# Four rotated products into the output product, and a negation on ScalarE, in the S5 scan of layer 0

## The chip, the cores and the metric
One Trainium2 chip, one core of it. The metric is the device time of one execution in microseconds (us), the median of several. Engines: TensorE (PE, with PEld its weight loads), VectorE (DVE), ScalarE (ACT), GpSimd (POOL) and SyncE (SP), which issues the DMAs.

## The reference
A two-layer trunk for 256 tokens of width 1024. The part that the change touches is the S5 mixer of layer 0: 32 groups of 64 complex states, a diagonal recurrence over the tokens, and an output product that takes the real part.

```python
step = jnp.exp(log_step)[:, None]
mag = jnp.exp(lr * step)
ar = mag * jnp.cos(li * step)
ai = mag * jnp.sin(li * step)
...
bu_r = jnp.einsum("bsgh,gph->sbgp", uf, bbr)
bu_i = jnp.einsum("bsgh,gph->sbgp", uf, bbi)
_, _, xr, xi = lax.associative_scan(_complex_combine, (a_r, a_i, bu_r, bu_i), axis=0)
y = (jnp.einsum("sbgp,ghp->bsgh", xr, c_re)
     - jnp.einsum("sbgp,ghp->bsgh", xi, c_im))
y = y + d_skip * uf
y = jax.nn.gelu(y.reshape(bsz, s, S5_WIDTH))
return y * jax.nn.sigmoid(y @ w_glu)
```

## The kernel before
The recurrence is solved in 16 steps (`for q in range(NQ)`), each for two groups, that is 128 states on the partitions and 256 tokens along the row. The complex decay is split into its size and its angle: the inputs are turned back by the angle of their token, a real scan with the size runs over real and imaginary part, and the result is turned forward again. The tables of cosines and sines lie in slots 4 and 5 of the weight ring. All engines run loops of their own over the same 16 steps and meet at semaphores.

- **TensorE.** `s5_in(q)` (L1417) writes the two inputs of a step into a bank, one step ahead. `s5_out(q)` (L1409) multiplies the two state parts with the output weights `ct` and adds them up in one bank over four steps; it waits for `re_ready` and `im_ready`. In iteration q the order is `s5_in(q+1)`, the turn of the previous adaLN row (`ada_turn`, L1313, after its copy on ScalarE and the previous row's sum on VectorE), `s5_out(q-2)`, in iterations 3 to 7 the products of the pooling mixer (L1280), and in iterations 4, 5, 7, 8, 10, 11, 13 and 14 (`ADA_AT`) the product of one adaLN weight tile (`ada_mm`, L1305).
- **VectorE.** Two products of the bank with the tables (L982), a sum and a difference of them (L985, L986), the two scans (L990) into `zz`, then `states(q-1)` (L972), which makes the imaginary part of the step before out of two of GpSimd's products; then, after an adaLN step, `mods` (L826, L829), and in steps 6, 10 and 14 `skip` (L967), which takes the finished bank of four steps. The scans wait until GpSimd is done with step q-2, since `zz` and `qq` have two buffers each.
- **GpSimd.** After both scans of a step, and after `s5_out(q-2)` for its buffer, two products of 128x512 (L531) give four rotated parts of 256 each, and one sum (L534) makes the real part of the state.
- **ScalarE.** Copies only: the pooling mixer's two (L665, L669), the adaLN row (`ada`, L585, which waits for `ada_mm`), and `gelu` (L674) behind `skip` in iterations 6, 10 and 14, with one table load ahead of the first.

The adaLN and the later weight tiles are issued by SP in the order of a list, each as soon as the last user of its ring slot is done; the slots of the tables are refilled after the last rotated product. After the 16 steps follow the last `skip` and `gelu`, the product of the gate (L1280, 32 records, "glu"), the output projection, and the feed-forward part of layer 0.

What a step leaves in `qq` before: with zr, zi the scanned parts and C, S the tables, `qq[k]` holds (zr, zi) times C for k=0 and times S for k=1, and the sum and difference of them are the two state parts.

## Time and profile before

| | |
|---|---|
| median of 3 runs | 1679.56 us (1677.16 to 1680.3) |
| profiled execution, its own time | 1678.3 us |
| span of the profiled execution | 1676.2 us |
| busy over the span | PE 92%, PEld 54%, DVE 26%, ACT 13%, POOL 6% |
| the chain that ended last | PE 80%, DMA 8%, DVE 6%, issue 4%, ACT 1% |
| chain from 81 to 151 us | VectorE, line after line of the scan loop |

The span is what the profiler saw of one execution; 2.1 us of the execution's own time lie around it. The shares of the whole span say little here, since the change lies in some 75 us of it. In that stretch the chain of waits runs through VectorE; ahead of it and behind it it runs through TensorE.

### The profile page before, as it was taken

The page shows a single profiled execution, that of the slowest core. Times are in us where ns is not written, and L with a number is a line of the kernel's source. Part 1 is how long each engine was busy: PE and PEld are TensorE (multiplying, and loading weights), DVE is VectorE, ACT ScalarE, POOL GpSimd, SP SyncE. Part 2 cuts the span into 40 slices and gives each one's busy share as a digit, 9 for nine tenths or more (in the row PEclk, how much of TensorE's full clock was granted, in tenths as well). Part 3 has the DMA queues.
Part 4 walks back from the last instruction along what each step waited for, and adds up shares of the span by engine and source line. Part 5 has one row for each costly group of instructions (what it writes and reads, how often), then busy time and mean ns, then how long its engine had stood idle before and what let it go on. Part 6 is the DMA issues. An engine that isn't in the chain of part 4 may idle for free.

```text
span 1676.2 us, 23905 instructions
## 1 busy us (share of the span) xinstructions
PE 1544.0 (92%) x10681; PEld 906.2 (54%) x10682; DVE 429.9 (26%) x895; ACT 215.0 (13%) x411; POOL 106.1 (6%) x129
## 2 busy tenths in 40 slices
PE   7887999999999999989999998999999889977975
PEld 5644487777588766546343353356666643423322
DVE  6796212232255455222000001010010010100202
ACT  3311300000321143220000000000000000000001
POOL 7164000000000011000000000000000000000000
PEclk9997999999999999998999999999999999999999
DMA  9576386664564403255999986999999969999996
GB/s 339 177 247 236 139 302 244 234 224 169 181 228 151 151 1 143 109 206 216 404 408 409 391 296 259 403 408 408 402 406 395 377 250 404 407 409 403 408 407 240
DMA packets 167297, 485.74 MB, mean 290 GB/s; under 512 B 12928, under 2 KB 15872, under 8 KB 167168
## 3 DMA queue, kind: packets, MB, share of 16 engines
q1 hardware_dynamic: 162624, 482.51, 75.4%
q8 instruction: 103, 1.69, 0.4%
q10 hardware_dynamic: 4544, 1.33, 0.4%
q14 instruction: 26, 0.21, 0.0%
HBM read 482.78 MB, written 1.05 MB: 289 GB/s over the span
## 4 chain that ended last, share of the span: by engine, by line
PE 80%; DMA 8%; DVE 6%; issue 4%; ACT 1%; POOL 0%; DVEq 0%; SPq 0%; POOLq 0%; ACTq 0%
PE bank L1753 26%; PE bank L1280 21%; PE bank L1784 13%; DMA ring<-in_moe_w_down 5%; PE bank L1483 5%; PE bank L1673 3%; DMA ring<-in_moe_w_gate 3%; PE bank L1593 3%; PE bank L1725 2%; PE bank L1287 1%; DVE arena L982 1%; PE bank L1765 1%; PE bank L1632 1%; DVE arena L990 1%; PE bank L1608 1%
## 5 line engine op out<-in xcount | busy, mean ns | idle before, releaser
L1753 PE MATMUL bank<-ring,arena 128*32 128x256 f32 (+3 forms) x3664 | 387.0, 432 | 42.1 <-issue 27.0
L1753 PEld LDWEIGHTS bank<-ring,arena 128*32 128x32 f32 (+1 forms) x3664 | 179.4, 121 | 238.6 <-issue 182.0
L1280 PE MATMUL bank<-arena,ring 128*128 128x256 f32 x1264 | 282.8, 384 | 1.4 <-ACT arena L674 1.0
L1280 PEld LDWEIGHTS bank<-arena,ring 128*128 128x128 f32 x1264 | 240.9, 193 | 34.4 <-ACT arena L674 1.7
L1784 PE MATMUL bank<-ring,arena 128*32 128x256 f32 (+1 forms) x1792 | 208.1, 459 | 16.1 <-DMA ring<-in_moe_w_down 15.3
L1202 DVE TENSOR_TENSOR arena<-arena,bank 128x512 f32<-128x512 f32 (+2 forms) x44 | 24.4, 577 | 658.6 <-PE bank L1753 658.6
L1784 PEld LDWEIGHTS bank<-ring,arena 128*32 128x32 f32 (+1 forms) x1792 | 87.4, 121 | 127.4 <-issue 90.8
L1753 PE MATMUL bank<-arena 128*32 128x256 f32 (+3 forms) x1200 | 116.1, 402 | 9.8 <-issue 4.0
L788 ACT ACTIVATE arena<-bank 128x512 f32<-128x512 f32 (+2 forms) x44 | 21.1, 508 | 645.5 <-PE bank L1765 549.1
L1753 PEld LDWEIGHTS bank<-arena 128*32 128x32 f32 (+1 forms) x1200 | 57.9, 121 | 65.8 <-issue 49.9
L1483 PE MATMUL bank<-ring,arena 128*128 128x512 f32 x176 | 76.9, 595 | 1.5 <-PE bank L1280 1.5
L1593 PE MATMUL bank<-ring,arena 128*128 128x512 f32 x128 | 59.4, 608 | 2.5 <-DVE hd L1098 2.5
L1483 PEld LDWEIGHTS bank<-ring,arena 128*128 128x128 f32 x176 | 33.0, 190 | 42.5 <-issue 42.5
L1673 PE MATMUL bank<-ring,arena 128*128 128x512 f32 x128 | 55.3, 593 | 0.0
L1020 DVE TENSOR_TENSOR arena<-arena,bank 128x256 f32<-128x256 f32 x22 | 9.3, 421 | 160.2 <-PE bank L1280 160.2
L1784 PE MATMUL bank<-arena 128*32 128x256 f32 (+1 forms) x336 | 43.2, 472 | 3.1 <-DMA arena<-in_moe_w_down 3.1
L531 POOL TENSOR_TENSOR arena<-arena,ring 128x512 f32<-128x512 f32 x32 | 41.5, 1316 | 67.0 <-DVE arena L990 59.6
L1188 DVE TENSOR_SCALAR arena<-bank,gs,mod 128x128 f32<-128x128 f32 x64 | 21.9, 404 | 84.7 <-PE bank L1280 84.7
L844 DVE SCALAR_TENSOR_TENSOR arena<-ring,cT,arena 128x512 f32<-128x512 f32 x56 | 42.1, 751 | 1.7
L1280 PE MATMUL bank<-ring,arena 128*128 128x512 f32 x96 | 42.0, 594 | 0.1
L546 POOL TENSOR_TENSOR arena<-arena,hd 128x256 f32<-128x256 f32 x16 | 10.2, 636 | 504.4 <-ACT arena L725 376.6
L556 POOL COPY arena<-arena 128x6 f32<-128x6 f32 x8 | 1.5, 188 | 638.3 <-DVE arena L1179 618.0
(274 smaller groups left out, 1240.5 us busy)
## 6 DMA issues: line engine op xcount, KB each, us to landing
ring<-in_moe_w_down SPq DMA_DIRECT2D x46, 2048.0 KB, 19.3
ring<-in_moe_w_up SPq DMA_DIRECT2D x45, 2048.0 KB, 23.6
ring<-in_moe_w_gate SPq DMA_DIRECT2D x41, 2048.0 KB, 23.7
ring<-in_ada_w SPq DMA_DIRECT2D x24, 2048.0 KB, 9.5
arena<-in_moe_w_gate SPq DMA_DIRECT2D x15, 2048.0 KB, 23.6
ring<-in_m_w_in SPq DMA_DIRECT2D x12, 2048.0 KB, 9.0
arena<-in_moe_w_up SPq DMA_DIRECT2D x11, 2048.0 KB, 23.6
arena<-in_moe_w_down SPq DMA_DIRECT2D x10, 2048.0 KB, 21.7
```

What stands on the lines that cost most here:

```text
L531: c.inc(g.tensor_tensor(qq[:, q % 2, k], zz[:, q % 2], tables[:, 1 - k, q:q + 1, :].broadcast_to([P, 2, TOK]), ALU.mult), "q_ready")
L788: ins = f(sg[:, b, 0:w], ps[b][:, 0:w], ACT.Silu)
L844: c.then(stt(o, w[:, kc], cT[:, kc, 0:1], o, ALU.mult, ALU.add), "ada_summed" if kc == KC - 1 else step)
L1188: ins = ts(hcur3[:, kc], bank(kc // 4, 4, P)[:, kc % 4], gs[:, kc:kc + 1], mod[:, 1, 3, kc:kc + 1], ALU.mult, ALU.add)
L1202: ins = tt(sg[:, b, 0:w], sg[:, b, 0:w], ps[2 + b][:, 0:w], ALU.mult)
L1280: ins = mm(out_, l, r, start=i == 0, stop=i == len(pairs) - 1, **kw)
L1483: ins = mm(ps[i][:, :], act_f[:, t % 2, j, P * b:P * b + P], w[:, j, HALF * h:HALF * h + HALF], start=t == 0 and j == 0, stop=t == 5 and j ...
L1593: ins = mm(ps[6 + zi % 2][:, :], hT[:, kc, P * b:P * b + P], w[:, kc], start=kc == 0, stop=kc == KC - 1)
L1673: ins = mm(ps[4 + i][:, :], yT1[:, 4 * t + j, P * b:P * b + P], w[:, j, HALF * h:HALF * h + HALF], start=t == 0 and j == 0, stop=t == 3 an ...
L1725: mm(ps[banks[i]][:, :], gates[:, P * (i // 2):P * (i // 2) + P], y_sb[:, HALF * (i % 2):HALF * (i % 2) + HALF], start=True, stop=True).th ...
L1753: ins = mm(ps[base + b // per][m * h:m * h + m, w * (b % per):w * (b % per) + w], hcur3[:, kc, m * b:m * b + m], sl[:, kc - half * rows, w ...
L1784: ins = mm(ps[4 + b // per][m * h:m * h + m, w * (b % per):w * (b % per) + w], actT[:, t % 2, b // per, n * (b % per) + i, m * q:m * q + m ...
```

## The change
`zz` becomes two buffers of three parts, (zr, zi, -zr), the third written by ScalarE (`negate`, an ACTIVATE Copy with scale -1). The first rotated product of GpSimd takes (zr, zi), the second (zi, -zr) and waits for the negation. The four results need no sum or difference any more: TensorE multiplies each with its weights and adds all four in the bank, four products a step where there were two. The sum on GpSimd (L534) and the difference on VectorE (L972) go, with their semaphores. `s5_out` waits for the two rotated products.

```diff
-        zz = area(16384, 2, 2, TOK)
+        zz = area(7424, 3, TOK), area(16384, 3, TOK)
...
                 for k in range(2):
-                    c.inc(g.tensor_tensor(qq[:, q % 2, k], zz[:, q % 2],
+                    if k:
+                        pool.wait_ge(s["neg_ready"], q + 1)
+                    c.inc(g.tensor_tensor(qq[:, q % 2, k], zz[q % 2][:, k:k + 2],
                                           tables[:, 1 - k, q:q + 1, :].broadcast_to([P, 2, TOK]), ALU.mult), "q_ready")
-                pool.wait_ge(s["q_ready"], 2 * q + 2)
-                c.inc(g.tensor_tensor(qq[:, q % 2, 0, 0], qq[:, q % 2, 0, 0], qq[:, q % 2, 1, 1], ALU.add), "re_ready")
...
+            def negate(q):
+
+                act.wait_ge(s["z_ready"], 2 * q + 1)
+                if q >= 2:
+                    act.wait_ge(s["q_ready"], 2 * (q - 1))
+                c.inc(f(zz[q % 2][:, 2], zz[q % 2][:, 0], ACT.Copy, scale=-1.0), "neg_ready")
             for q in range(NQ):
+                if q:
+                    negate(q - 1)
...
                 if q in (6, 10, 14):
                     gelu((q - 6) // 4)
+            negate(NQ - 1)
             gelu(3)
...
-            def states(q):
-
-                dve.wait_ge(s["q_ready"], 2 * q + 2)
-                c.inc(tt(qq[:, q % 2, 0, 1], qq[:, q % 2, 0, 1], qq[:, q % 2, 1, 0], ALU.subtract), "im_ready")
...
-                if q:
-                    states(q - 1)
...
-                pe.wait_ge(s["re_ready"], q + 1)
-                pe.wait_ge(s["im_ready"], q + 1)
+                pe.wait_ge(s["q_ready"], 2 * (q + 1))
...
                 for i in range(2):
-                    ins = mm(ps[4 + m % 2][:, 0:TOK], ct[:, q, i], z[:, 0, i], start=q % 4 == 0 and i == 0,
-                             stop=q % 4 == 3 and i == 1)
+                    for k, part in enumerate((z[:, 0, i], z[:, 1, i])):
+                        ins = mm(ps[4 + m % 2][:, 0:TOK], ct[:, q, i], part, start=q % 4 == 0 and i == 0 and k == 0,
+                                 stop=q % 4 == 3 and i == 1 and k == 1)
```

On ScalarE `negate(q-1)` stands at the head of iteration q, so `negate(q)` is queued behind all that iteration q holds. The rows from iteration 3 to the first `gelu` (iteration 6) and one row beyond, before, where L665 and L669 are the pooling mixer's copies and L585 the copy of an adaLN row:

```order
L665 ACTIVATE arena<-bank0 128x256
L669 ACTIVATE arena<-bank0,cols 128x256
L665 ACTIVATE arena<-bank1 128x256
L585 ACTIVATE arena<-bank6 128x512
L669 ACTIVATE arena<-bank1,cols 128x256
L665 ACTIVATE arena<-bank0 128x256
L585 ACTIVATE arena<-bank6 128x512
L669 ACTIVATE arena<-bank0,cols 128x256
L665 ACTIVATE arena<-bank1 128x256
L674 ACT_TABLE_LOAD
L674 ACTIVATE arena<-arena 128x256
L669 ACTIVATE arena<-bank1,cols 128x256
```

and now, from the copy of iteration 4 on:

```order
L585 ACTIVATE arena<-bank6 128x512
L680 ACTIVATE arena<-arena 128x256
L669 ACTIVATE arena<-bank1,cols 128x256
L665 ACTIVATE arena<-bank0 128x256
L585 ACTIVATE arena<-bank6 128x512
L680 ACTIVATE arena<-arena 128x256
L669 ACTIVATE arena<-bank0,cols 128x256
L665 ACTIVATE arena<-bank1 128x256
L674 ACT_TABLE_LOAD
L674 ACTIVATE arena<-arena 128x256
L680 ACTIVATE arena<-arena 128x256
L669 ACTIVATE arena<-bank1,cols 128x256
```

Each L680 is a negation. Those of steps 4 and 5 stand behind the adaLN copies (L585) of iterations 4 and 5, that of step 6 behind the first `gelu`. No table load is added.

On GpSimd the first two steps and the start of the third, before:

```order
L531 TENSOR_TENSOR arena<-arena,ring 128x512 [waits z_ready,tab_sin,band_ready]
L531 TENSOR_TENSOR arena<-arena,ring 128x512
L534 TENSOR_TENSOR arena<-arena 128x256 [waits q_ready]
L531 TENSOR_TENSOR arena<-arena,ring 128x512 [waits z_ready]
L531 TENSOR_TENSOR arena<-arena,ring 128x512
L534 TENSOR_TENSOR arena<-arena 128x256 [waits q_ready]
L531 TENSOR_TENSOR arena<-arena,ring 128x512 [waits y_mm,z_ready]
```

and now:

```order
L533 TENSOR_TENSOR arena<-arena,ring 128x512 [waits z_ready,tab_sin,band_ready]
L533 TENSOR_TENSOR arena<-arena,ring 128x512 [waits neg_ready]
L533 TENSOR_TENSOR arena<-arena,ring 128x512 [waits z_ready]
L533 TENSOR_TENSOR arena<-arena,ring 128x512 [waits neg_ready]
L533 TENSOR_TENSOR arena<-arena,ring 128x512 [waits y_mm,z_ready]
```

Two instructions a step in place of three, the second with a wait of its own. On TensorE iteration 4 (`s5_in(5)`, `s5_out(2)`, pooling, `ada_mm`), before:

```order
L1417 MATMUL bank3<-arena,ring 128x256 [waits bu_used]
L1417 MATMUL bank3<-arena,ring 128x256
L1409 MATMUL bank4<-arena 128x256 [waits im_ready,re_ready]
L1409 MATMUL bank4<-arena 128x256
L1280 MATMUL bank0<-arena 128x256 [waits pool_in_ready]
L1280 MATMUL bank1<-arena 128x256 x2
L1305 MATMUL bank6<-ring,cT 32x512 [waits ring_full2,ada_copied]
```

and now:

```order
L1419 MATMUL bank3<-arena,ring 128x256 [waits bu_used]
L1419 MATMUL bank3<-arena,ring 128x256
L1411 MATMUL bank4<-arena 128x256 [waits q_ready]
L1411 MATMUL bank4<-arena 128x256 x3
L1282 MATMUL bank0<-arena 128x256 [waits pool_in_ready]
L1282 MATMUL bank1<-arena 128x256 x2
L1307 MATMUL bank6<-ring,cT 32x512 [waits ring_full2,ada_copied]
```

The adaLN product, for which ScalarE's copy waits, stands behind two more products of 128x256.

## Rows read from the trace of the kernel before

**Rows 1.** Windows: length; busy (count) of PE, PEld, DVE, ACT, POOL; clock; DMA.
```profile
82.30:151.50 69.20, 53.02 (x288) 30.85 (x286) 67.62 (x108) 10.63 (x20) 43.65 (x40) 0.93 0.66 231
```

**Rows 2.** Timeline of DVE: start, length (us), line, operation, [idle before <-releaser].
```profile
86.19 1.68 DVE L990 TENSOR_TENSOR_SCAN arena<-hd,arena 128x256 f32<-128x256 f32 x2
...
108.86 0.40 DVE L972 TENSOR_TENSOR arena<-arena 128x256 f32<-128x256 f32 x1
109.18 1.41 DVE L982 TENSOR_TENSOR arena<-bank,ring 128x512 f32<-128x512 f32 x2
110.62 1.29 DVE L985 TENSOR_TENSOR arena<-arena 128x256 f32<-128x256 f32 x1
111.84 0.95 DVE L986 TENSOR_TENSOR arena<-arena 128x256 f32<-128x256 f32 x1
112.82 1.27 DVE L990 TENSOR_TENSOR_SCAN arena<-hd,arena 128x256 f32<-128x256 f32 x2
...
114.53 1.02 DVE L829 TENSOR_TENSOR mod<-modraw,cols 128x4 f32<-128x4 f32 x1
...
116.91 0.94 DVE L985 TENSOR_TENSOR arena<-arena 128x256 f32<-128x256 f32 x1
...
118.22 1.27 DVE L990 TENSOR_TENSOR_SCAN arena<-hd,arena 128x256 f32<-128x256 f32 x2
```

**Rows 3.** Timeline of POOL beside them.
```profile
109.03 2.61 POOL L531 TENSOR_TENSOR arena<-arena,ring 128x512 f32<-128x512 f32 x2 [2.00 <-DVE arena L990]
111.71 0.79 POOL L534 TENSOR_TENSOR arena<-arena 128x256 f32<-128x256 f32 x1
114.23 2.54 POOL L531 TENSOR_TENSOR arena<-arena,ring 128x512 f32<-128x512 f32 x2 [1.73 <-issue]
116.84 0.72 POOL L534 TENSOR_TENSOR arena<-arena 128x256 f32<-128x256 f32 x1
```

**Rows 4.** Timeline of DVE, step 15, which comes late enough to find POOL idle.
```profile
147.38 0.47 DVE L967 SCALAR_TENSOR_TENSOR arena<-arena,cols,bank 128x256 f32<-128x256 f32 x1
...
149.21 0.55 DVE L985 TENSOR_TENSOR arena<-arena 128x256 f32<-128x256 f32 x1
149.69 0.41 DVE L986 TENSOR_TENSOR arena<-arena 128x256 f32<-128x256 f32 x1
150.13 1.27 DVE L990 TENSOR_TENSOR_SCAN arena<-hd,arena 128x256 f32<-128x256 f32 x2
```

**Rows 5.** Timeline of PE, iteration 5.
```profile
93.92 1.03 PE L1409 MATMUL bank<-arena 128*128 128x256 f32 x4
94.78 1.46 PE L1280 MATMUL bank<-arena 128*128 128x256 f32 x6
96.17 1.92 PE L1305 MATMUL bank<-ring,cT 128*32 128x512 f32 x16
```

**Rows 6.** Timeline of ACT, iterations 5 and 6.
```profile
98.16 0.60 ACT L585 ACTIVATE arena<-bank 128x512 f32<-128x512 f32 x1 [1.50 <-PE bank L1305]
...
102.97 1.28 ACT L674 ACT_TABLE_LOAD   x1
105.42 0.42 ACT L674 ACTIVATE arena<-arena 128x256 f32<-128x256 f32 x1 [1.16 <-DVE arena L967]
```

**Rows 7.** Timeline of DVE and PE at the end of the loop and behind it.
```profile
147.60 0.63 PE L1313 MATMUL bank<-ident,arena 128*128 128x128 f32 x4 [3.37 <-DVE mod L829]
...
154.17 0.98 DVE L972 TENSOR_TENSOR arena<-arena 128x256 f32<-128x256 f32 x1 [1.30 <-POOL arena L531]
155.29 2.04 PE L1409 MATMUL bank<-arena 128*128 128x256 f32 x4 [1.38 <-DVE arena L972]
...
158.36 9.12 PE L1280 MATMUL bank<-arena,ring 128*128 128x256 f32 x32 [1.02 <-ACT arena L674]
```

**Rows 8.** Windows of PE: length, busy (count), clock, DMA share, GB/s.
```profile
148.00:149.00 1.00, 1.00 (x7) 0.84 0.00 0
162.00:163.00 1.00, 1.00 (x5) 0.83 1.05 387
```

More of the change, by code:

```diff
@@ L279, in hybrid_trunk @@
             xn_ready turned hT_low hT_high gs_ready u_mm u_ready pool_mm pool_in_ready pool_out_mm pool_out
-            bu_mm bu_used z_ready q_ready re_ready im_ready y_mm yskip ys_ready glu_mm glu_sig yT_ready gg_ready grow_mm grow_ready
+            bu_mm bu_used z_ready neg_ready q_ready y_mm yskip ys_ready glu_mm glu_sig yT_ready gg_ready grow_mm grow_ready
             sq_done rg_ready root_in root_done xroot_done out_mm x_ready dve_step             f_mm f_silu f_act
@@ L989, in _ @@
                 for k in range(2):
-                    c.inc(v.tensor_tensor_scan(zz[:, q % 2, k], prm[:, MAG, q:q + 1].broadcast_to([P, TOK]), t[:, k, 0],
+                    c.inc(v.tensor_tensor_scan(zz[q % 2][:, k], prm[:, MAG, q:q + 1].broadcast_to([P, TOK]), t[:, k, 0],
                                                0.0, ALU.mult, ALU.add), "z_ready")
-                if q:
-                    states(q - 1)
                 if q - 1 in ADA_AT:
@@ L998, in _ @@
                 dve.wait_ge(s["z_ready"], 2 * (q + 1))
-            states(NQ - 1)
             skip(3)
```

## Prediction

> **What bounds the kernel now.** The reader first looks at the chain of waits, which goes through VectorE from 81 to 151 us, and at the windows of that stretch: of 69.20 us VectorE is busy 67.62, TensorE 53.02, GpSimd 43.65, ScalarE 10.63 [rows 1]. So the scan loop ends when VectorE ends, and TensorE has 16 us to spare.
>
> Next comes the timeline of VectorE, to see of what a step consists. I call T(q) the end of step q's second scan. T(3) is 87.87 and T(15) 151.40 [rows 2, 4], 63.5 us for 12 steps, 5.3 each. From T(7)=108.95 to T(8)=114.09 it takes: L972 up to 109.18, the table products (L982) 1.44, L985 1.22, L986 0.98, the scans 1.27 [rows 2]. Where GpSimd is idle, L985 takes 0.48 and L986 0.44 [rows 4]. The difference is waiting: L985, queued at 110.62, ends as GpSimd's second product does (109.03 + 2.61 = 111.64), and L986 as its sum does (111.71 + 0.79 = 112.50) [rows 2, 3]. L829, a sum of 4 columns, takes 1.02 and ends with the first product; L982, which reads a bank, doesn't wait at all. So an operation of VectorE with both inputs in SBUF waits for the instruction that GpSimd has running, and the port is handed over between two instructions. This is the rule of the Trainium skill ("SBUF — State Buffer", Who interferes with whom): such an instruction contends with GpSimd's reads, and who comes first blocks the other for the whole instruction. These rows agree (1.29 where 0.48 is free).
>
> **Part 1: L534 and L972 go.** A step without `mods` is then: table products up to T+1.4; L985 waits for the second product, which ends at T+2.7, and is done at T+2.9; L986 0.44, scans 1.3: 4.63 in place of 5.14, a gain of 0.51. A step with `mods`: L829 waits for the first product up to T+1.4 whether L972 stood ahead of it or not, so L972's time there was hidden; table products to 2.8, when GpSimd is done; L985 0.48, L986 0.44, scans 1.3: 5.03 against 5.40 (114.09 to 119.49), a gain of 0.37, which is L534's block alone. Twelve intervals, seven with `mods`: 5 x 0.51 + 7 x 0.37 = 5.1 us, if nothing takes their place.
>
> **Part 2: the negation.** The trace has no such instruction; the nearest are L674 at 0.42 for 128x256 (SBUF to SBUF) and L585 at 0.60 for twice as much [rows 6]; I take 0.42 and 0.05 for each handover. It can start after the first scan, at T-0.65, and GpSimd needs it at T+1.35. It costs nothing as long as ScalarE is free by T+0.9. Queued ahead of it are:
> - `gelu` in steps 6, 10 and 14, behind `skip`. With `mods` (6, 14) `skip` ends at T+1.9 (0.47, rows 4), gelu at 2.35, the negation at 2.8, the second product at 4.15. L985, ready at 3.3, waits up to 4.3, and the step takes 6.05: 0.65 more than before instead of 0.37 less. Two of them cost 2 x 1.0 = 2.0. Step 10 has no `mods`, its negation is 0.05 late: 0.1.
> - the adaLN copy in eight steps, which waits for TensorE.
>
> **Part 3: TensorE.** `s5_out` takes 0.86 for two products (93.92 to 94.78) and `s5_in`, of the same shape and number, as much [rows 5]; four products take 1.72. Sixteen more times 0.86 are 13.8 us in a stretch where 16 are idle, so the averages say that it fits, but order counts. In its favour, `s5_out(q-2)` needn't wait for L972, which ran only after the next scans, so it may start 2.3 us earlier. After the long input projection TensorE starts behind: it ends `s5_out(0)` at 83.8, then s5_in 0.86, s5_out 1.72, pooling 0.86, s5_in, s5_out(2) to 89.8, pooling 1.4, `ada_mm` 1.85 up to 93.05 [durations from rows 5]. The copy ends at 93.75 and step 4's negation at 94.15, with T(4)=92.55: late by 0.25. The next round is 0.95+0.45+1.72+1.3+1.85, so `ada_mm` ends at 99.35, copy 100.05, negation 100.45, with T(5)=97.15: the second product is late by 1.9. VectorE has done its table products, L985 and L986 at 100.9; the product then takes the port up to 102.2, and the scans end at T(6)=103.35 (before 103.54, so the gain up to there is 0.2). Then step 6 with its gelu, whose table load (1.28, rows 6) now comes later, since it stands behind a pooling copy that ends at 104.25: negation 106.35, T(7)=109.65, 0.7 behind the kernel before. GpSimd starts step 7 late for the same reason: T(8)=114.35, 0.25 behind.
>
> From here TensorE keeps up (copy of step 8 ends at T(8), of 11 at T(11)-1.0), and the gains of part 1 add up: steps 8 and 9 to 124.4 (0.5 ahead), 10 to 129.1 (0.95), 11 and 12 to 139.16 (1.7), 13 to 143.8 (2.2), 14 with gelu to T(15)=149.8, **1.6 ahead**.
>
> **Part 4: the tail.** Before, GpSimd's products end 2.65 after T(15), L972 takes 0.98 (it waits for L534) and 1.1 in all, then s5_out(15) 2.04 at half clock up to 157.35 [rows 7], 5.95 after T(15). Now L972 goes and the products double: 149.8 + 2.9 = 152.7, and then between 1.9 (full clock) and 3.8 (half). Before, the clock fell to half at about 148.7, just after a gap of 3.37 us that ended at 147.60, and rose at about 162.3 [rows 7, 8]. Now TensorE idles from 142.1 to 145.3, works 4 us with a half us between, and idles 3.0 again, so I take half clock: end 156.5, **0.85 ahead**. The gate product took 9.12 for 32 records [rows 7], where at the full rate of 0.215 a record (four in 0.86, rows 5) it takes 6.9: a clock that rises earlier by virtue of the longer s5_out(15) gives back 0 to 2.2; I take 1.1.
>
> Sum: 0.85 + 1.1 = 1.95. Nothing behind absorbs it: the output projection and the feed-forward part are TensorE's chain, their tiles are issued when a slot or the tables come free, which moves by as much. The adaLN tiles of this stretch land before use (`ring_full` releases no matmul here). Start of the loop: the negations of steps 0 and 1 stand behind the copies L679 at 73.3 and 81.0; GpSimd gets them by 82.0, VectorE's step 3 starts at 82.3 with its bank anyway, and s5_out(1) at 84.6. Cost nothing, and if that cover failed, 0.3 us. `zz` at 7424 covers nothing that is alive.
>
> The profiled execution took 1678.3 (span 1676.2), 1.26 below the median; taken off its own time the sum gives 1676.3, taken off the median **1677.6**, which I forecast.
>
> **Rivals.**
> 1. *The clock holds through the tail.* s5_out(15) 1.9 instead of 3.8 and the gate product at full rate: 1.9 + 1.1 more, a gain of 5.0, **1674.6**. For it: TensorE has more work in every gap. Against it: the 3.0 us gap just ahead. Chance 0.20.
> 2. *A scan goes ahead of the late product.* In steps 5 and 6 I let the product have the port after L986. If the first scan, queued right behind, keeps it, the scans are through 1.15 earlier in step 5 and about 0.9 in step 6: a gain of 4.0, **1675.6**. The rows show the port handed to a waiting VectorE instruction between two of GpSimd's, never the reverse. Chance 0.15. By the Trainium skill (the section named above) the first to start holds the port, which leaves this case open, since both are ready at once.
> 3. *The negation is late in all adaLN steps.* The copy must end by T+0.9. By my account step 8 has 1.0 us of margin and step 11 1.9. If TensorE falls to half clock for some us, as it did somewhere in the loop before (mean clock 0.93, rows 1), or the round is 1 us longer than summed, the second product moves in front of the scans instead of lying beside the table products, at 6.2 - 5.03 = 1.2 a step; six more steps cost 7.2, a loss of 5.2, **1684.8**. It decides from a copy that ends later than T+0.9. Against it: TensorE no longer waits for L972. Chance 0.13.
> 4. *The blocks only move.* Each of VectorE's small operations finds a product running anyway, because GpSimd starts late for want of its buffer: loop even, tail 0.75 worse, **1680.3**. Chance 0.07.
>
> **How the numbers follow.** Forecast 0.45, held inside 1676.2 to 1680. A measurement can tell about 0.2% (3.4 us) from no change. Faster by more than that (below 1676.2): rivals 1 and 2, 0.35, and 0.02 of the forecast's edge: 0.37. Slower (above 1682.9): rival 3, 0.13. The rest, 0.50, is within. The range goes from rivals 1 and 2 together (1679.56 - 7.05 = 1672.5) to 1682.5, which leaves out most of rival 3 and a little below: 0.18 in all.
>
> **What would show it.** In the timeline of the changed kernel: steps without `mods` of 4.6 us and with them of 5.0 (part 1); steps 5, 6 and 14 of 6 us or more, with the second product away from the first by 1 to 2 us (parts 2, 3); T(15) near 149.8; s5_out(15) of 3.8 at a granted clock of 0.5. Wrong: a gap between the two products in steps 8 to 13 (rival 3), a last s5_out of 1.9 (rival 1), a scan running while GpSimd's second product is ready and waits (rival 2), or L985 above 0.5 in the steps with `mods` (part 1).

## The result and the profile after

The changed kernel took **1669.11 us** in the median of 5 runs (1665.53 to 1670.13), the kernel before 1679.56 in 5 runs of the same series (1677.16 to 1681.11): ratio 0.9939, interval 0.9928 to 0.9950, so faster by 0.6%. A second series gave 1671.17 (1668.82 to 1671.77) against 1679.6, ratio 0.9948 (0.9931 to 0.9965). The forecast of 1677.6 had the sign of its sum right and the size wrong by 8.5 us, and its range (1672.5 to 1682.5) did not reach the result. The profiled execution took 1668.35, with a span of 1666.5 against 1676.2 before. One run of this study, one of the five of the kernel with the sum alone, took 2157.58 us at a mean granted clock of 0.70; its ratio leaves it out.

Windows of the scan loop in the kernel after, from the table products of step 3 up to the end of step 15. The columns are those of [rows 1]: length; busy (count) of PE, PEld, DVE, ACT, POOL; clock; DMA share; GB/s.

```profile
85.66:150.80 65.14, 61.65 (x352) 41.77 (x350) 63.42 (x96) 15.15 (x33) 34.30 (x27) 1.00 0.70 245
```

VectorE is still the engine that is always busy (63.42 of 65.14), GpSimd has lost its third instruction, and the granted clock is 1.00 where it was 0.93 [rows 1]. The loop from T(3) to T(15) takes 59.50 where it took 63.53.

Timeline of VectorE in the kernel after: from T(7) to T(8) without `mods`, and from 130.96 on T(11) to T(12), with `mods`. Columns as in [rows 2].

```profile
112.36 1.42 DVE L987 TENSOR_TENSOR arena<-bank,ring 128x512 f32<-128x512 f32 x2
113.81 1.37 DVE L990 TENSOR_TENSOR arena<-arena 128x256 f32<-128x256 f32 x1
115.11 0.41 DVE L991 TENSOR_TENSOR arena<-arena 128x256 f32<-128x256 f32 x1
115.56 1.27 DVE L995 TENSOR_TENSOR_SCAN arena<-hd,arena 128x256 f32<-128x256 f32 x2
...
130.96 1.26 DVE L838 TENSOR_TENSOR mod<-modraw,cols 128x4 f32<-128x4 f32 x1
132.15 1.40 DVE L987 TENSOR_TENSOR arena<-bank,ring 128x512 f32<-128x512 f32 x2
133.58 0.42 DVE L990 TENSOR_TENSOR arena<-arena 128x256 f32<-128x256 f32 x1
133.92 0.42 DVE L991 TENSOR_TENSOR arena<-arena 128x256 f32<-128x256 f32 x1
134.38 1.27 DVE L995 TENSOR_TENSOR_SCAN arena<-hd,arena 128x256 f32<-128x256 f32 x2
```

L990 and L991 are the lines that were L985 and L986. L838 is the sum of 4 columns that was L829, and L987 the table products, L982 before. Without `mods`, the first still waits for GpSimd's second product (1.37, where [rows 2] have 1.29) and the second runs free at 0.41 where it took 0.98, since no sum follows on GpSimd. With `mods`, both are free at 0.42, and it is the sum of 4 columns (L838) that waits, 1.26. The steps last 4.50 and 4.79, where they lasted 5.14 and 5.40.

Timeline of TensorE at the end of the loop in the kernel after, to be held against [rows 7].

```profile
142.33 1.92 PE L1307 MATMUL bank<-ring,cT 128*32 128x512 f32 x16
146.46 0.63 PE L1315 MATMUL bank<-ident,arena 128*128 128x128 f32 x4 [2.21 <-DVE mod L838]
146.92 3.93 PE L1411 MATMUL bank<-arena 128*128 128x256 f32 x16
153.34 2.00 PE L1411 MATMUL bank<-arena 128*128 128x256 f32 x8 [2.48 <-POOL arena L533]
156.42 7.17 PE L1282 MATMUL bank<-arena,ring 128*128 128x256 f32 x32 [1.09 <-ACT arena L674]
```

The last `s5_out` has 8 records in 2.00, where it had 4 in 2.04, and the gate product takes 7.17 where it took 9.12. TensorE runs at 2.4 GHz here throughout. The windows of TensorE from 120 to 165 us show it (length, busy (count), granted clock, DMA share, GB/s), first of the kernel after:

```profile
120.00:165.00 45.00, 37.93 (x214) 1.00 0.71 249
```

and the same of the kernel before:

```profile
120.00:165.00 45.00, 33.71 (x150) 0.77 0.58 202
```

**Where the 9.7 us of span went.** I use three marks: T(0), the end of the first step's scans; T(15); and F, the first matmul of the feed-forward part behind the gate, at which the code is again the same in both kernels.

| us | T(0) | T(0) to T(3) | T(3) to T(15) | T(15) to F | T(0) to F | F to the end |
|---|---|---|---|---|---|---|
| before | 68.9 | 18.96 | 63.53 | 54.45 | 136.94 | 1470.4 |
| before, second trace | 71.1 | 18.97 | 63.53 | 54.43 | 136.93 | 1470.5 |
| after | 72.3 | 18.96 | 59.50 | 51.25 | 129.71 | 1464.5 |
| after, second trace | 71.9 | 18.95 | 59.50 | 51.24 | 129.69 | 1467.8 |

The head of the program, which the change leaves alone, happened to be 3.35 longer in the first trace of after (T(0) lies between 68.6 and 72.3 in all traces of this study). The loop gives 4.0, the tail 3.2, together 7.2 us, repeated to 0.02. The rest, 5.9 in the first pair of traces and 2.7 in the second, lies in code that is the same in both kernels. So there are two questions: why the changed stretch gives 7.2 and not the 1.95 forecast, and why the code behind it got shorter.

### The profile page after: what moved, and what is told of

Its sections match the earlier page's. It is cut to its first block, busy times and chain, and to the rows that moved or that the text cites. A ratio compares the mean times of both kernels' runs of the same rounds, so it can differ in the third digit from the quotient of the medians.

```text
span 1666.5 us, 24017 instructions
## 1 busy us (share of the span) xinstructions
PE 1547.8 (93%) x10745; PEld 913.0 (55%) x10746; DVE 421.0 (25%) x879; ACT 220.3 (13%) x427; POOL 93.5 (6%) x113
## 4 chain that ended last, share of the span: by engine, by line
PE 77%; DMA 8%; issue 2%; DVE 2%; ACT 1%; POOL 0%; DVEq 0%; SPq 0%
PE bank L1755 26%; PE bank L1282 20%; PE bank L1786 13%; DMA ring<-in_moe_w_down 5%; PE bank L1485 5%; PE bank L1675 3%; DMA ring<-in_moe_w_gate 3%; PE bank L1595 3%; PE bank L1727 2%; PE bank L1767 1%; PE bank L1634 1%; PE bank L1610 1%; PE bank L1330 1%; PE bank L1296 0%; PE bank L1475 0%
## 5 line engine op out<-in xcount | busy, mean ns | idle before, releaser
L1485 PEld LDWEIGHTS bank<-ring,arena 128*128 128x128 f32 x176 | 33.0, 190 | 42.5 <-issue 42.5
L1675 PEld LDWEIGHTS bank<-ring,arena 128*128 128x128 f32 x128 | 24.2, 191 | 29.6 <-issue 29.6
L1595 PEld LDWEIGHTS bank<-ring,arena 128*128 128x128 f32 x128 | 23.8, 196 | 26.8 <-issue 26.8
```

Of the source, the lines that this page charges most:

```text
L1485: ins = mm(ps[i][:, :], act_f[:, t % 2, j, P * b:P * b + P], w[:, j, HALF * h:HALF * h + HALF], start=t == 0 and j == 0, stop=t == 5 and j ...
L1595: ins = mm(ps[6 + zi % 2][:, :], hT[:, kc, P * b:P * b + P], w[:, kc], start=kc == 0, stop=kc == KC - 1)
L1675: ins = mm(ps[4 + i][:, :], yT1[:, 4 * t + j, P * b:P * b + P], w[:, j, HALF * h:HALF * h + HALF], start=t == 0 and j == 0, stop=t == 3 an ...
```

## The experiments

**One add at a time, and none.** The first kernel leaves only the sum to TensorE. It is the kernel before with

```diff
-                pool.wait_ge(s["q_ready"], 2 * q + 2)
-                c.inc(g.tensor_tensor(qq[:, q % 2, 0, 0], ..., ALU.add), "re_ready")
...
-                for i in range(2):
-                    ins = mm(..., ct[:, q, i], z[:, 0, i], ...)
+                for n, (i, part) in enumerate(((0, z[:, 0, 0]), (0, z[:, 1, 1]), (1, z[:, 0, 1]))):
+                    ins = mm(..., ct[:, q, i], part, ...)
```

> Only GpSimd's sum goes: TensorE takes its two terms as two products (three a step), VectorE keeps the difference (L972), no negation. Both theories: L985 and L986 lose the block by the sum, steps without the adaLN sum 4.5, with it 4.8, nothing is late in steps 5, 6 and 14, so T(15)-T(3) about 57 (59.5 in the changed kernel, 63.5 before). Rival B: total 1679.6 less 6.6 less 1, about 1672. Theory A: the same with 2 to 6 more if no half-clock stretch falls into 120 to 165, 1666 to 1670.

It took 1672.07 in the median of five runs, ratio 0.9954 (0.9938 to 0.9971). T(3) to T(15) is 58.04, shorter than in the changed kernel, and T(0) to F 128.47. Timeline of VectorE in it:

```profile
110.53 1.28 DVE L983 TENSOR_TENSOR arena<-arena 128x256 f32<-128x256 f32 x1
111.73 0.41 DVE L984 TENSOR_TENSOR arena<-arena 128x256 f32<-128x256 f32 x1
...
113.88 1.03 DVE L827 TENSOR_TENSOR mod<-modraw,cols 128x4 f32<-128x4 f32 x1
...
116.28 0.42 DVE L983 TENSOR_TENSOR arena<-arena 128x256 f32<-128x256 f32 x1
```

The second leaves only the difference to TensorE:

```diff
-                if q:
-                    states(q - 1)
...
+                for n, (i, part) in enumerate(((0, z[:, 0, 0]), (1, z[:, 0, 1]), (1, z[:, 1, 0]))):
```

> Only VectorE's difference goes: GpSimd keeps its sum, TensorE takes the two terms of the imaginary part as two products (three a step), without the negation, so that one sign is wrong; read up to the feed-forward part only. By the ledger L972 was hidden behind GpSimd's products in the steps with the adaLN sum and in the others too (L985 waits for the second product up to T+2.8 anyway), and L986 still waits for the sum: T(15)-T(3) 62.5 to 63.5, and only the tail gains 1. If L972 was on the path in every step: 0.3 a step less, 59.5.

1682.17 in one run (one sign of its imaginary part is wrong, so only its loop is read); the loop takes 62.18, only 1.35 less than before. Timeline of VectorE in it, a step without `mods`:

```profile
112.18 1.39 DVE L981 TENSOR_TENSOR arena<-arena 128x256 f32<-128x256 f32 x1
113.49 0.95 DVE L982 TENSOR_TENSOR arena<-arena 128x256 f32<-128x256 f32 x1
114.47 1.27 DVE L986 TENSOR_TENSOR_SCAN arena<-hd,arena 128x256 f32<-128x256 f32 x2
```

With the sum still on GpSimd, the second of VectorE's two adds waits for it (0.95); with the sum gone it doesn't (0.41). VectorE's own instruction, the difference, was nearly free: its time went into a wait that came anyway. So the gain of the loop is the sum's, an instruction of 0.79 us on an engine that isn't the bound [rows 3].

The third has neither add nor negation:

```diff
-                    if k:
-                        pool.wait_ge(s["neg_ready"], q + 1)
-                    c.inc(g.tensor_tensor(qq[:, q % 2, k], zz[q % 2][:, k:k + 2],
+                    c.inc(g.tensor_tensor(qq[:, q % 2, k], zz[q % 2][:, 0:2],
...
-                if q:
-                    negate(q - 1)
```

> The changed kernel without the negation: GpSimd's second product takes the same two parts as the first (one sign of the four is wrong) and waits for nothing on ScalarE. If the lateness of the negation behind the adaLN copies and the gelus costs what the ledger says, steps 5, 6 and 14 fall from 5.8, 6.1 and 5.8 to 4.8 or 5.2 and T(15)-T(3) from 59.5 to about 57: total 1666.5. If a late product costs nothing because the scans find another place, 59.5 and 1669 stay.

Its loop takes 57.52. So the adds are worth 63.53 - 57.52 = 6.0, and the negation takes 59.50 - 57.52 = 2.0 of it back. (Its total of 1651.55 can't be held against the others, since the router behind sees other values and sends other tokens: it ran 8898 matmul records where the kernel after has 10745.)

The 6.0 are not the whole of what the adds blocked. Timeline of GpSimd in this kernel, step 6:

```profile
104.96 2.68 POOL L531 TENSOR_TENSOR arena<-arena,ring 128x512 f32<-128x512 f32 x2 [3.39 <-PE bank L1400]
```

In steps 6, 8 and 9 GpSimd starts late, 1.2, 0.6 and 0.8 us after the scans, since TensorE's `s5_out` (L1400), twice as long now, still holds its buffer. From T(6), T(8) and T(9) to the next it takes 5.46, 4.92 and 5.03, where a step with `mods` takes 4.80, and 5.18 with `skip` too, when nothing is late: in part of this faster loop the bound has moved to TensorE.

**When the negation comes.** The rows say why it takes 2.0. Timeline of GpSimd in the kernel after, of which the row at 109.90 belongs to step 6 and the two before to step 5:

```profile
100.44 1.27 POOL L533 TENSOR_TENSOR arena<-arena,ring 128x512 f32<-128x512 f32 x1 [1.67 <-DVE arena L995]
103.89 1.75 POOL L533 TENSOR_TENSOR arena<-arena,ring 128x512 f32<-128x512 f32 x1 [2.18 <-ACT arena L680]
...
109.90 1.30 POOL L533 TENSOR_TENSOR arena<-arena,ring 128x512 f32<-128x512 f32 x1 [2.36 <-ACT arena L680]
```

and of ScalarE in the same kernel:

```profile
102.91 0.60 ACT L585 ACTIVATE arena<-bank 128x512 f32<-128x512 f32 x1 [1.50 <-PE bank L1307]
103.40 0.41 ACT L680 ACTIVATE arena<-arena 128x256 f32<-128x256 f32 x1
...
107.80 1.28 ACT L674 ACT_TABLE_LOAD   x1
109.09 0.42 ACT L674 ACTIVATE arena<-arena 128x256 f32<-128x256 f32 x1
109.42 0.40 ACT L680 ACTIVATE arena<-arena 128x256 f32<-128x256 f32 x1
```

The second product waits 2.18 for the negation (L680), which stands behind the adaLN copy (L585) and with it behind TensorE; one step later it waits 2.36, behind the gelu and its table load, and in step 14 it waits 1.24 behind the gelu. It also waits 0.43 in step 4 (T(4) to T(5) takes 4.63 where 4.50 is usual), and 3.87 and 5.24 in steps 0 and 1, which cost nothing: T(0) to T(3) is 18.96 as before. In all other steps the two products follow each other. The experiment puts the negation ahead of the copy:

```diff
             for q in range(NQ):
-                if q:
-                    negate(q - 1)
+                negate(q)
...
-            negate(NQ - 1)
```

> The changed kernel with the negation of step q at the head of iteration q on ScalarE, ahead of the pooling copies, the adaLN copy and gelu, instead of at the head of iteration q+1. If its queueing is what makes steps 5, 6 and 14 long: they fall to 4.8 and 5.2, T(15)-T(3) about 57, total 1666.5 to 1667. If the pooling copies that now wait for the scan hold TensorE's pooling products back: up to 2 us of that are lost again around steps 4 to 6.

The loop takes 57.53, all 2.0 back, as the kernel without negation has it. Timeline of ScalarE in it, step 5: the negation (L680) is through long before the copy (L585).

```profile
99.64 0.42 ACT L680 ACTIVATE arena<-arena 128x256 f32<-128x256 f32 x1 [2.56 <-DVE arena L993]
102.86 0.60 ACT L585 ACTIVATE arena<-bank 128x512 f32<-128x512 f32 x1 [1.50 <-PE bank L1305]
```

On VectorE in the same kernel the scans that follow are not held up:

```profile
103.72 1.27 DVE L993 TENSOR_TENSOR_SCAN arena<-hd,arena 128x256 f32<-128x256 f32 x2
```

And yet it took 1670.71 (ratio 0.9954, 0.9937 to 0.9971), no better than the changed kernel, and T(0) to F is 130.50 against 129.71. The tail has lost more than the loop gained, as the timeline of TensorE in this kernel shows:

```profile
145.03 0.63 PE L1313 MATMUL bank<-ident,arena 128*128 128x128 f32 x4 [1.36 <-DVE mod L836]
145.50 3.62 PE L1409 MATMUL bank<-arena 128*128 128x256 f32 x16
151.33 2.46 PE L1409 MATMUL bank<-arena 128*128 128x256 f32 x8 [2.21 <-POOL arena L533]
154.88 9.46 PE L1280 MATMUL bank<-arena,ring 128*128 128x256 f32 x32 [1.09 <-ACT arena L674]
```

TensorE falls to 1.2 GHz at 152.7 for 6.8 us, and the gate product takes 9.46, although both gaps ahead (1.36 and 2.21) are shorter than in the kernel after (2.21 and 2.48), where the clock held. This is the case that my part 4 had forecast, in another kernel.

**Filling the last gap.** Idle products on TensorE, which wait for nothing and write a bank nobody reads:

```diff
             s5_out(NQ - 2)
+            pe.wait_ge(s["pool_out"], 4)
+            stay_warm(8, 0)
             s5_out(NQ - 1)
+            stay_warm(3, 0)
```

on top of the edit before.

> The negation first (as in e5), and idle products of TensorE only where it waits at the end: eight (2 us) ahead of the last s5_out, in e5's gap of 2.2, and three behind it. If e5's half-clock stretch on the gate product comes from that gap, it is gone and nothing is late: loop 57.5, T(15) to the feed-forward part 51.3, first scan to feed-forward part 127.8, total 2 under the changed kernel. If products in the gap don't keep the clock: 54.0 and 130.5, as e5.

```profile
147.98 1.95 PE L1287 MATMUL bank<-ident 128*128 128x128 f32 x16
150.37 1.99 PE L1409 MATMUL bank<-arena 128*128 128x256 f32 x8 [0.44 <-POOL arena L533]
152.20 0.83 PE L1287 MATMUL bank<-ident 128*128 128x128 f32 x6
153.46 7.17 PE L1280 MATMUL bank<-arena,ring 128*128 128x256 f32 x32 [0.42 <-ACT arena L674]
```

The timeline of TensorE shows the clock held, the gate product at 7.17 again, and T(0) to F at 127.76, the shortest of the study and 1.95 less than the changed kernel. Its total of 1669.04 (1667.07 to 1670.44; ratio 0.9943, 0.9926 to 0.9959) can't be told from the changed kernel's all the same. An earlier form put idle products into iterations 12 to 15 too:

> The changed kernel with the negation first (as in e5) and six idle products of TensorE before the adaLN turn of iterations 12 to 15, eight before the last s5_out and three behind it, into a bank that nobody reads. e5 had the shorter loop (57.5) but a half-clock stretch of 6.8 us on its last products and the gate (54.0 from T(15) to the feed-forward part, 51.3 in the changed kernel). If TensorE's idleness there is the cause of the stretch, it is gone: loop 57.5 to 58, T(15) to the feed-forward part 51.0 to 51.5, total 2 under the changed kernel, 1667. If the stretch comes at that place whatever TensorE does: 1670.5, as e5.

It took 1671.49 (0.9957, 0.9940 to 0.9973), with 58.20 in the loop and 130.16 from T(0) to F. A miss of mine: the idle products delay an `s5_out`, GpSimd finds its buffer late, and step 14 takes 5.85. Timeline of GpSimd in it:

```profile
141.51 2.70 POOL L533 TENSOR_TENSOR arena<-arena,ring 128x512 f32<-128x512 f32 x2 [3.49 <-PE bank L1409]
```

**The clock alone.** Is it the adds, or is it that TensorE has more to do and so keeps its clock? The kernel before with every product of `s5_out` done twice:

```diff
                 for i in range(2):
-                    ins = mm(..., ct[:, q, i], z[:, 0, i], start=q % 4 == 0 and i == 0,
-                             stop=q % 4 == 3 and i == 1)
+                    for k in range(2):
+                        ins = mm(..., ct[:, q, i], z[:, 0, i], start=q % 4 == 0 and i == 0 and k == 0,
+                                 stop=q % 4 == 3 and i == 1 and k == 1)
```

> The kernel before, with TensorE's output products of each scan step doubled in number (the same product added twice, so the S5 part of the output is twice too large) and nothing else. Theory A (a good half of the gain of the change is the clock: more products in the gaps keep TensorE at full clock through the end of the loop, and the code behind meets fewer half-clock stretches): loop unchanged, T(15)-T(3) 63.5, no half-clock stretch between 120 and 165, gate product 7.2 instead of 9.1, total 1673 to 1677. Rival B (the gain is the two removed adds and what they blocked, the clock is a by-product of the shorter loop): 0 to 2 us above the kernel before, 1679.5 to 1681.5, with the half-clock stretch at the end of the loop still there.

The loop is exactly that of before (63.53). The timeline of TensorE at the tail:

```profile
157.66 1.97 PE L1410 MATMUL bank<-arena 128*128 128x256 f32 x8 [1.68 <-DVE arena L972]
160.65 7.17 PE L1280 MATMUL bank<-arena,ring 128*128 128x256 f32 x32 [1.02 <-ACT arena L674]
```

Twice the products in less time than before, and the gate product at 7.17: with more work in the loop the clock falls less. Between 110 and 170 us it is at half for 3.4 us (from 150.1), where before has 20.5. T(15) to F is 52.63 where before has 54.45. So of the 7.2 us the clock accounts for 1.8 to 1.95 (9.12 - 7.17) at the gate product, and the loop for 4.0. The 1.3 at its end come from the adds, since the last `s5_out` starts 2.62 after T(15) instead of 3.89; there the clock just pays for the doubled products (8 records in 2.00 at full clock, 4 in 2.04 at half). (The total, 1696.22, isn't comparable, for the router's reason above.)

**The code behind.** Now the second question. Both kernels once more, unchanged, beside each other on one chip:

> The kernel before once more, for a second trace of it. The half-clock stretches between 120 and 165 belong to the idle gaps of TensorE in the loop and come again (theory A). Those behind 205 us: if the 5.8 us that the changed kernel gained there in its trace were the chance of one execution, the stretch from the feed-forward part's first product to the end takes 1464 to 1470 here; if they belong to the change, it takes 1470 again.

> The changed kernel once more, for a second trace and for a ratio taken beside the other kernels of this chip: 0.994. Chance of one execution: from the feed-forward part to the end 1464 to 1470; belonging to the change: 1464.5 again. The loop takes T(15)-T(3) 59.5 and its first scan to the feed-forward part 129.7 again, unless a half-clock stretch falls on the gate product (then 132).

They gave 1680.69 and 1671.17; the marks are in the table above. The changed stretch repeats to 0.02, the code behind to 0.2 (before) and 3.3 (after).

Then the same kernel with its later code started later, by idle products ahead of the gate product:

```diff
             pe.wait_ge(s["bu_used"], 2 * NQ)
+            stay_warm(9, 0)
             w = slot(arrived(AT["glu", 0]), 4, HALF)
```

and with 18 in place of 9, and 18 in the kernel before.

> The changed kernel with 9 idle products (18 records, 2.0 us at full clock) between the scan loop and the gate product, that is a delay of 2 us and nothing else. If the length from the feed-forward part to the end depends only on the code, it is that of the changed kernel and the total is 2 us longer. If it depends on the instant at which that code starts (1464.6 and 1467.8 in two executions of the changed kernel, 1470.4 and 1470.5 before), it lands anywhere from 1464 to 1471, with its half-clock stretches at other places of the code.

> As e6 with 18 idle products, 4.0 us. Same alternatives: total 4 us longer, or a later part anywhere from 1464 to 1471.

> The kernel before with 18 idle products ahead of the gate product. If the later part's 1470.4 belongs to the kernel before, it stays 1470.4. If it belongs to the instant at which it starts, it may be up to 6 us shorter here, and the total grows by less than the 4 us. The idle products also take the half-clock stretch that lay on the gate product before (9.1), so that it falls to 7.2.

The results did not order themselves by the delay: 1679.6 with 2 us, 1672.5 with 4 us, and 1688.0 for before with 4 us, one run each. So I repeated the first two and added the fourth corner, with ten, five and ten runs:

> The changed kernel with a delay of 2 us ahead of the gate product, now in several executions. Instant of the start: the median is 5 or more above the changed kernel's 1669 to 1671, as the one execution at 1679.6 was. Scatter: median 1671 to 1673.

> The changed kernel with a delay of 4 us, in several executions. Instant of the start: the median lies under that of the 2 us delay, at 1671 to 1674. Scatter: median 1673 to 1675, 2 above that of the 2 us delay.

> The kernel before with a delay of 2 us at the same place (9 idle products; with the clock at half there up to 4 us of it, and 2 given back on the gate product). Instant of the start: the later part departs from 1470.4 by 2 or more in the trace and the median isn't 2 above 1679.5. Scatter: median 1681 to 1682, later part 1470.4.

| | no delay | 2 us | 4 us |
|---|---|---|---|
| after: T(0) to F | 129.7 | 131.7 | 133.7 |
| after: F to the end, each trace | 1464.5, 1467.8 | 1475.1, 1476.7 | 1464.7, 1471.0 |
| after: median | 1669.1, 1671.2 | 1681.6 (1677.5 to 1682.5) | 1674.9 (1670.9 to 1677.8) |
| before: T(0) to F | 136.9 | 138.8 | 141.5 |
| before: F to the end, each trace | 1470.4, 1470.5 | 1472.5 | 1473.3 |
| before: median | 1679.4 | 1680.7 (1678.2 to 1684.5) | 1688.0 (one run) |

A delay of 2 us, made of 18 records on TensorE, costs the changed kernel 10.5 to 12.5 us, and eats the whole gain: its ratio to before is 1.0005 (0.9996 to 1.0015). A delay of 4 us costs 4 to 6. In the kernel before, a delay of 2 us (1.9 from T(0) to F) costs 1.2 in the median.

Where does it lose them? Held matmul by matmul against after, the 2 us kernel lags by 1.7 from the feed-forward part up to 460 us, by 3.5 when the experts' products begin at 772, by 8.9 when their first block ends at 793, and by 8.9 to 13.9 from there on. The block is worth a look. Timeline of TensorE in the kernel after:

```profile
771.94 20.82 PE L1755 MATMUL bank<-ring,arena 128*64 128x512 f32 x96 [1.91 <-issue]
```

and in the kernel with 2 us of delay, ten-run series:

```profile
775.42 1.04 PE L1756 MATMUL bank<-ring,arena 128*64 128x512 f32 x3 [2.07 <-issue]
778.89 22.79 PE L1756 MATMUL bank<-ring,arena 128*64 128x512 f32 x93 [2.42 <-issue]
```

The same 96 products, but after three of them the engine pauses for 2.42 and goes on at half its rate: the weight loads come every 0.85 us up to 783, where they come every 0.43 in after. The half rate is the clock, as the window of TensorE in the same trace shows:

```profile
777.00:783.80 6.80, 4.91 (x12) 0.50 0.01 2
```

Pause and clock make 5.4 us, some 2.8 and 2.6 of it (93 records take 20.17 at the rate of after, and 22.79 here), and none of it is made good. The DMA queue has next to nothing to move in that stretch (DMA share 0.01); from 801 to 900 us its share is 1.03 and TensorE is busy 95.85 of 99 us, so neither has room to catch up. The earlier trace of this kernel has the same pause at the same record (2.18 after three). "Issue" means that the profile shows nothing that the engine waits for. Over the whole later part (205 to 1640 us) the line with most of TensorE's waits (total, times, longest) is, first for after:

```profile
PE bank L1755 <- issue: 26.4, 11, 6.1
```

then before:

```profile
PE bank L1753 <- issue: 31.0, 12, 6.7
```

then after with 2 us of delay:

```profile
PE bank L1756 <- issue: 34.0, 13, 6.8
```

The second traces of the three have 28.7, 30.9 and 33.0. Added up over all lines of TensorE, and beside the time for which the granted clock was at half between F and 1655 us:

| each trace | F to the end | waits "issue", all lines | clock at half |
|---|---|---|---|
| after | 1464.5, 1467.8 | 29.7, 30.2 | 34.1, 44.4 |
| after, 2 us | 1476.7, 1475.1 | 36.2, 35.5 | 51.2, 51.2 |
| after, 4 us | 1464.7, 1471.0 | 32.0, 30.7 | 34.1, 51.2 |
| before | 1470.4, 1470.5 | 32.3, 32.5 | 44.4, 44.4 |
| before, 2 us | 1472.5 | 34.1 | 44.4 |
| before, 4 us | 1473.3 | 35.5 | 44.4 |

Neither column orders the traces alone, but both together do: at the same time at half clock the later part is the longer, the longer the pauses. The two traces with 4 us are one and the same kernel, and differ by 6.3 us, with 17.1 us more at half clock in the longer: part of the length isn't the program's at all.

And some of these pauses have a place that isn't one of the algorithm. Counting TensorE's matmul records in the trace, pauses of 1.4 to 2.5 us stand at records 6690 and 6817 in the kernel after; in the one with 18 records more ahead, at 6691 and 6818, other products by then; in the one with 36 more, at 6818 and 6945; in before, which has 64 fewer, at 6682 and 6810; and in the kernel before with the products of `s5_out` doubled, which has those 64 too, at 6683 and 6810. A second pair stands at 9009 and 9137 in after and at 9010 and 9138 with 18 and with 36 records more. They are 127 or 128 records apart and stay at their number, to within 8, while the code moves past them by up to 100. The Trainium skill ("Runtime: NRT & Kernel Launch", Instruction fetch mechanics) says that instructions are fetched in blocks of 256; a matmul record here comes with a weight load, so 128 records make one block, and the trace agrees with the distance. The Trainium skill calls the crossing "mostly hidden"; these rows show up to 2.5 us at one, and there the measurement decides.

The trace also has the transfers of a DMA queue of the kind "instruction", in packets of 16 KB. The DMA view of the kernel with 2 us of delay (ten-run series), from 776.46 to 778.89, the pause after the third record, holds one of them and nothing else (packets, MB, share):

```profile
q8 instruction: 1, 0.02, 2.4%
```

It lands at 777.47, and TensorE goes on 1.42 us later. So it is for most of them: in the 14 traces of kernels that leave the router's input as it is, 143 pauses "issue" behind F are longer than 1.3 us, and 113 of them end 1.2 to 1.7 us after such a packet has landed, though only some 97 packets come in these 1470 us. Against them stand some ten such pauses a kernel, so most packets come without one. That these pauses are waits for instructions is what the times say; what a packet holds isn't shown, and the remaining pauses (2.25 us ahead of the experts, for one) are open.

So an edit that adds 64 records to TensorE's stream, as this change does, or 18, as my delay does, moves the later products against these places, besides moving them in time. For the extra pause two traces tell the one from the other. The kernel with 2 us, in its one run, begins the experts' block at 773.91 and pauses after three records. The kernel with 4 us, in its one run, begins it at 773.98, and its timeline of TensorE has no pause:

```profile
773.98 22.52 PE L1756 MATMUL bank<-ring,arena 128*64 128x512 f32 x96 [2.45 <-issue]
```

(22.52 and not 20.82 because the clock is at half for 3.4 us from 774.0.) The second traces, at 775.42 and 778.01, say the same. So that pause goes with the place in the stream and not with the instant; what sets the time at half clock is open.

## Why the prediction was wrong

**What was right.** VectorE bounds the loop and goes on doing so. The sum on GpSimd, and not VectorE's own instruction, is what cost. Where the negation costs, it is late in steps 5, 6 and 14, and a little in step 4, behind the copy and the gelu, by the path that I had named: I had step 5's second product late by 1.9, and it waited 2.18. Rival 3, the negation late in all steps, and rival 4 didn't occur. Rival 3 was near, though: it was to decide from a copy that ends later than T+0.9, and I had given step 8 a margin of 1.0 us. That copy ended at 117.99, which is T(8)+1.16, and the negation at 118.29, just when GpSimd's first product of the step was through (116.97 to 119.63 for two). There was no margin left, and that it held was luck.

**Part 1, sizes: 5.1 forecast, 6.0 measured.** I took L985 and L986 where free at 0.48 and 0.44, from step 15 [rows 4], where GpSimd wasn't idle, as its timeline in the kernel before shows:

```profile
148.75 0.72 POOL L534 TENSOR_TENSOR arena<-arena 128x256 f32<-128x256 f32 x1
```

The sum ran up to 149.47, and L985 had started at 149.21. Start to start the two take 0.34 and 0.46 when free (133.58, 133.92, 134.38). Steps without `mods` come to 4.50 where I had 4.63, and gain 0.63 each instead of 0.51: 3.2 in five of them. Steps with `mods` come to 4.79 where I had 5.03, but by the kernel without negation only four of the seven are near it: step 6 takes 5.46 and step 9 5.03, with GpSimd waiting for its buffer, and step 14 5.18, with `skip` ahead of the table products. The seven gain 2.9, where I had 2.6.

**Part 2 with part 3, sizes: 3.5 taken back, 2.0 measured.** T(5) to T(6) took 5.83 (I had 6.2), the next 6.14 (6.3), and T(14) to T(15) 5.77 (6.0). Rival 2 came true in part in step 5: after the late negation the first scan had the port first. GpSimd's product, ready at 103.89, took 1.75 instead of 1.27, and the two scans together 2.30 instead of 1.27, as the second waited for the product. In step 6 the product was first, at 109.90, and both scans waited. Timeline of VectorE in the kernel after:

```profile
103.89 2.30 DVE L995 TENSOR_TENSOR_SCAN arena<-hd,arena 128x256 f32<-128x256 f32 x2
...
110.10 2.23 DVE L995 TENSOR_TENSOR_SCAN arena<-hd,arena 128x256 f32<-128x256 f32 x2
```

The same loop in the four traces with a delay behind it shows that rival 2 isn't what made the difference. There the product goes first in step 5, as I had let it; GpSimd in the first kernel with 4 us:

```profile
103.93 1.27 POOL L533 TENSOR_TENSOR arena<-arena,ring 128x512 f32<-128x512 f32 x1 [2.17 <-ACT arena L680]
```

The scans, ready at 103.93 too, take 2.39, T(5) to T(6) takes 5.92, and T(3) to T(15) is 59.49 to 59.53 all the same. So who goes first is worth 0.09 us in the step and nothing in the loop, and most of what the 6.2 had too much was again the free L985 and L986.

The loop as a whole: I had 61.93 for T(3) to T(15) (87.87 to 149.8), it took 59.50. That is 2.43 us of the error.

**Part 4, the step that failed.** "So I take half clock": s5_out(15) at 3.8. It took 2.00, at full clock, and ended 4.63 after T(15) where before it had ended 5.95 after; I had 6.7. That is 2.07 us. The gate product gave 1.95 where I took 1.1: 0.85 more. This is rival 1 (1.9 and 1.1 more, it said), to which I gave 0.20. Against it I had set a gap of 3.0 us just ahead; there was one of 2.48, behind one of 2.21, with 4 us of work between, and the clock held. In the kernel with the negation first it fell behind gaps of 1.36 and 2.21. So neither the gap nor its neighbours told which way it goes, and on these runs 0.20 was too little: the gate product was at the full rate (7.17) in after and in the kernels with the sum alone, without negation, with doubled products and with idle products, and slow in before (9.12), with the difference alone (9.89) and with the negation first (9.46). The doubled products show that the work in the loop matters; what decides between after and negation first is open.

2.43 + 2.07 + 0.85 and the 1.95 forecast make 7.3, against 7.2 measured from T(0) to F. The remaining 3.2 us of the error in the total (8.5 - 5.3) lie behind F.

**"Nothing behind absorbs it."** Nothing did, but the sentence took for granted that the rest keeps its length. It doesn't: F to the end was 1470.4 before and 1464.5 and 1467.8 after. Hence the further 1 to 3 us of the two medians (10.4 and 8.4 against 7.2). Taken over all three delays, with each delay subtracted, the kernels are 1670.1, 1679.6 and 1670.9 after (mean 1673.5), and 1679.4, 1678.8 and 1683.4 before (mean 1680.5): a difference of 7.0, with one of the six numbers from a single run. The three of after scatter by 9.5 us, so this agrees with the 7.2 of the stretch and can't prove it; F to the end, averaged in the same way over the traces, is 1470.0 after and 1472.1 before. What the change itself is shown to be worth is the 7.2 us of its stretch, and what is measured beyond it belongs to where this version of the stream happens to lie and to the clock of the single execution. In the second pair of traces the clock behind F was at half for 44.4 us in both kernels (the stretch at the very end left out), and the waits "issue" of all lines differ by 2.3 (32.5 and 30.2) of the 2.7 us. In the first pair they differ by 2.6 (32.3 and 29.7) of the 5.9, and the clock was at half for 44.4 against 34.1 us. So in the one pair it is nearly all in the pauses, in the other half in the pauses and the rest, by all signs, in the clock. Rivals 1 and 2 together, the lower end of my range, gave 7.05, which is this figure, but by chance: rival 1 came true, rival 2 was worth nothing, and the sizes of parts 1 and 2 made up for it. A range for the total would have needed some 4 us more on either side.

## What to carry to other kernels

- When two engines share a port, count what each instruction on the engine that is *not* the bound blocks on the one that is. The sum on GpSimd, 0.8 us a step, was nearly the whole gain (5.5 of 6.0); taking an instruction off the busy engine itself gave 1.35.
- A new wait is dangerous where it stands behind work that waits for a third engine. Two lines' difference in ScalarE's order decided 2.0 us of the loop, and the order that was best for the loop lost them at the tail until the gap there was filled.
- A comparison below 1% of a long, fully unrolled program should be made at marks inside it (the stretch that changed, to a point where the code is the same again) and with the start of the rest shifted by a few us. The stretch repeated to 0.02 us; the total moved by up to 12 us for 2 us of idle products.

## What the runs showed of the hardware

- The same later code takes 1464.5 to 1476.7 us, and 1464.7 and 1471.0 in two executions of one kernel. Pauses of TensorE without a releaser and its time at half clock go with it. Some of the pauses stand at fixed numbers of its stream, 127 or 128 records apart (6690 and 6817; 6691 and 6818; 6818 and 6945), and 113 of 143 end 1.2 to 1.7 us after a 16 KB packet of the queue "instruction" has landed. One of them, with the half clock behind it, cost 5.4 us that weren't caught up (775 to 801 in the kernel with 2 us of delay).
- The granted clock doesn't follow from the last gap. It held behind gaps of 2.21 and 2.48 us and fell behind 1.36 and 2.21, with 3.6 to 3.9 us of work between them in both.
- A sum of 4 columns on VectorE, both inputs in SBUF, takes up to 1.27 us beside a product of GpSimd and 0.16 without, nearly as long as one of 256 columns (1.37 and 0.42): it waits for the product, whatever its own size. Two instructions that read a bank (L987, 1.40 for both) are not held up.
- If a scan of VectorE and a product of GpSimd come ready within 0.01 us of each other, either can go first: in step 5 the scan did in two traces (the product took 1.75, the scans 2.30), and the product in four (1.27 and 2.39).
